# Output projection's last tile in two column quarters, a shorter expert choice, and rows of experts 1 to 11 gathered by DMA

## The chip, the cores and the metric

The kernel runs on one core of one Trainium2 chip. The metric is the device time of one execution in microseconds (us), taken as the median of repeated runs. Lower is better.

## The reference, cut to what matters

One layer of a hybrid decoder on 512 prompt tokens and 32 decode tokens (544 rows of width 1024, all float32). Attention and pooling branches are merged, then comes the output projection, a norm, a routed mixture of 32 experts of width 512 (top group of 4, then the best 2 of its 8 experts), and the residual sum:

```python
x = x + merged @ w['w_out']
hn = rms_norm(x, w['norm_ffn_g'])
g_w, g_idx = lax.top_k(softmax(hn @ w_route_group + b_g), 1)
top_l, top_i = lax.top_k(e_logits[group g_idx], 2)
comb = g_w * softmax(top_l)
# every token goes through its two experts:
y = (silu(xb @ w_gate[e]) * (xb @ w_up[e])) @ w_down[e]
x = x + sum over the two experts of comb * y
```

The weights of all 32 experts (6 MB each, 201 MB in all) have to come in from HBM, and an expert has some 34 of the 1088 token slots.

## The kernel before, in words

The program is written by hand with one instruction stream for each engine: TensorE (PE), VectorE (DVE), ScalarE (ACT), GpSimd (POOL) and SyncE (SP), which issues the loads of weights. Semaphores order the streams, and each stream runs strictly in the order of the code. Three stages matter here.

**Output projection and routing.** The token rows are five tiles: the decode tile first, then four prompt tiles of 128 rows (`ORDER`). The 1024 output columns are taken in halves of 512: half number 0 is the whole decode tile, halves 1 to 4 are the left halves of the four prompt tiles, 5 to 8 the right halves, and half 8 is called `LAST`. For each half PE runs `half_out` (8 products of 128 x 128 by 128 x 512 float32, 16 instructions in the trace, since a float32 product is two), DVE adds the residual (`add_out`), PE transposes the sum (`turn`), ACT or DVE copies the transpose out of PSUM, and PE forms routing logits from it (`route`). When both halves of a tile are there, DVE takes the reciprocal of the norm (`inverse2`), and then `choice` picks the group and the two experts by some twenty small dependent operations. From the choice PE computes each token's place in its experts' lists (`tile_ranks`), and DVE makes from it `mark`, one-hot tables `hot` and `hit` (`hits`); `tile_list` makes the lists of row numbers, `list_i`. The finished sums are also written to a table in HBM, `x2_rows`, and to the output `y`.

**How an expert gets its rows.** For experts in `SELECTED` PE multiplies a one-hot matrix with all token rows, which are kept in SBUF split into bfloat16 parts (`select`, 24 products of 512 columns and two float32 products), ACT copies the result out (`stage_x`) and PE transposes it (`turn_x`). For experts in `GATHERED` (2 to 8 before) POOL issues an indirect DMA that reads the rows of `x2_rows` by `list_i` (`gather_x`), and PE transposes what landed (`turn_gathered`). The row vector is then scaled by DVE (`take_x`). POOL's first gather waits until all of `x2_rows` is written (`base_written`) and the lists are there (`rows_listed`).

**Experts.** Each expert has three weight chunks of 2 MB: two for gate and up (`gate_up`), one for `down`. There are 96 chunks, and a ring of ten buffers (`CHUNK_AT`) in SBUF. SP issues chunk n + 10 once PE has used chunk n. Chunks 0 to 6 are issued when the projection begins, 7 to 9 when the projection's last data leave the places that the chunks overwrite. Chunks 10 and 11 are issued in four pieces each, as expert 0's first eight products free the buffers of chunks 0 and 1. POOL adds each expert's result to `y` by an indirect DMA (`add_y`). The part of a loop on DVE that follows expert 10 is a hardware loop.

## Time and profile before

| what | value |
|---|---|
| median of 3 runs | 976.71 us (975.9 to 978.06) |
| profiled execution | 975.49 us, of which the span of instructions is 973.7 us |
| PE busy | 935.4 us, 96% |
| DVE busy, ACT busy | 402.7 us, 241.4 us |
| HBM traffic | 260 MB, 268 GB/s over the span |

Times in the rows below are us from the span's start. PE's matmuls are pipelined, so their busy times overlap and a busy engine isn't one at its peak. "PEld" is PE's loading of weights. A wait is named by what released it.

### The profile page before, as it was taken

How to read it: one execution, taken by the hardware profiler on the slowest of the kernel's cores; microseconds unless marked ns; L12 is line 12 of the kernel's file. 1: busy time of each engine (PE TensorE's matmuls, PEld its weight loads, DVE VectorE, ACT ScalarE, POOL GpSimd, SP SyncE). 2: the span in 40 equal slices, each digit the busy share in tenths (PEclk: the TensorE clock that was granted, in tenths of full speed). 3: DMA queues.
4: the chain of work that ended last, by engine and by line, in shares of the span. 5: the costliest groups of instructions: out<-in, count | busy, mean ns of one | idle time of the engine just before them, and what ended most of it. 6: DMA issues, size and time to landing. Idle time of an engine off the chain costs nothing.

```text
span 973.7 us, 12332 instructions
## 1 busy us (share of the span) xinstructions
PE 935.4 (96%) x4804; PEld 506.4 (52%) x4804; DVE 402.7 (41%) x916; ACT 241.4 (25%) x600; POOL 70.6 (7%) x79
## 2 busy tenths in 40 slices
PE   5999999999999999999989999999999999999996
PEld 4555777777678888855444333333333333333331
DVE  4589688687543345553661242111111112111111
ACT  4432554454533100032221111111111111111111
POOL 0100001000000000002101111101101010110101
PEclk9999999999999999999999999999999999999999
DMA  9620412112112226369269999999999999999995
GB/s 330 217 87 24 149 55 84 44 44 87 44 44 86 87 87 229 140 255 409 113 221 385 393 393 415 423 418 417 422 416 423 419 415 424 417 423 420 425 416 181
DMA packets 33848, 255.17 MB, mean 262 GB/s; under 512 B 8241, under 2 KB 11569, under 8 KB 18792
## 3 DMA queue, kind: packets, MB, share of 16 engines
q1 hardware_dynamic: 28912, 242.45, 61.6%
q0 software_dynamic: 4880, 11.94, 4.4%
q8 instruction: 39, 0.64, 0.3%
q14 instruction: 17, 0.14, 0.0%
HBM read 245.91 MB, written 14.58 MB: 268 GB/s over the span
## 4 chain that ended last, share of the span: by engine, by line
PE 71%; DMA 20%; DVE 5%; ACT 1%; issue 1%; SPq 1%; POOL 0%; POOLq 0%; DVEq 0%; ACTq 0%
PE ps L1983 25%; DMA arena<-in_w_gu 19%; PE ps L2301 14%; PE ps L2328 7%; PE ps L1921 6%; PE ps L2142 4%; PE ps L2227 4%; PE ps L2068 1%; DMA arena<-in_x 1%; PE ps L2042 1%; PE ps L1999 1%; PE ps L2025 1%; PE ps L2271 1%; PE ps L2311 1%; PE ps L2302 1%
## 5 line engine op out<-in xcount | busy, mean ns | idle before, releaser
L1983 PE MATMUL ps<-arena 128*128 128x272 f32 x1120 | 266.7, 394 | 2.7 <-DVE arena L1395 1.0
L2301 PE MATMUL ps<-arena 128*64 128x512 f32 x512 | 229.7, 597 | 10.2 <-DMA arena<-in_w_gu 10.1
L1983 PEld LDWEIGHTS ps<-arena 128*128 128x128 f32 x1120 | 208.9, 190 | 52.3 <-issue 7.1
L2302 PE MATMUL ps<-arena 128*64 128x512 f32 x512 | 229.7, 597 | 0.0
L828 ACT ACTIVATE arena<-ps 128x272 f32<-128x272 f32 (+5 forms) x181 | 86.2, 483 | 364.7 <-PE ps L1983 167.6
L2301 PEld LDWEIGHTS ps<-arena 128*64 128x64 f32 x512 | 66.2, 137 | 141.5 <-issue 114.8
L1721 DVE SCALAR_TENSOR_TENSOR arena<-arena,list_w,ps 64x512 f32<-64x512 f32 x32 | 24.0, 749 | 217.9 <-ACT arena L1099 217.8
L2227 PE MATMUL ps<-arena 128*64 128x512 bf16 (+2 forms) x600 | 81.7, 421 | 0.9 <-DVE arena L1636 0.9
L1921 PE MATMUL ps<-arena 128*128 128x512 f32 (+1 forms) x192 | 74.1, 544 | 7.0 <-DVE arena L1187 7.0
L1099 ACT ACTIVATE arena<-ps,list_w 64x512 f32<-64x512 f32 x32 | 21.8, 682 | 202.3 <-PE ps L2302 202.2
L786 POOL DMA_INDIRECT out_y<-arena,list_i x32 | 45.2, 1414 | 362.4 <-DVE arena L1728 327.8
L2302 PEld LDWEIGHTS ps<-arena 128*64 128x64 f32 x512 | 66.2, 137 | 2.8 <-issue 2.8
L1717 DVE TENSOR_TENSOR arena<-ps,g_ffn 128x512 f32<-128x512 f32 x32 | 22.2, 692 | 100.0 <-PE ps L2271 94.3
L2328 PE MATMUL ps<-arena 128*64 128x512 f32 x256 | 61.1, 599 | 1.0 <-ACT arena L828 1.0
L2328 PE MATMUL ps<-arena,const 128*64 128x512 f32 x256 | 61.0, 598 | 0.5 <-ACT const L828 0.5
L2142 PE MATMUL ps<-arena 128*128 128x512 f32 x128 | 59.4, 602 | 0.0
L2227 PEld LDWEIGHTS ps<-arena 128*64 128x64 bf16 (+2 forms) x600 | 36.5, 116 | 40.6 <-issue 16.5
L1921 PEld LDWEIGHTS ps<-arena 128*128 128x128 f32 x192 | 38.1, 203 | 36.3 <-issue 33.7
L1728 DVE COPY arena<-ps 64x512 f32<-64x512 f32 x32 | 21.9, 683 | 49.9 <-PE ps L2328 49.9
L2142 PEld LDWEIGHTS ps<-arena 128*128 128x128 f32 x128 | 22.7, 190 | 21.7 <-issue 21.5
L928 ACT ACTIVATE arena<-arena,a_stat 128x256 f32<-128x256 f32 (+1 forms) x64 | 30.0, 471 | 14.9 <-DVE a_stat L1449 14.7
L2328 PEld LDWEIGHTS ps<-arena,const 128*64 128x64 f32 x256 | 16.9, 136 | 30.3 <-issue 29.4
(264 smaller groups left out, 772.2 us busy)
## 6 DMA issues: line engine op xcount, KB each, us to landing
arena<-in_w_gu SPq DMA_DIRECT2D x62, 2048.0 KB, 44.8
arena<-in_w_ed SPq DMA_DIRECT2D x30, 2048.0 KB, 47.1
arena<-in_w_pair SPq DMA_DIRECT2D x20, 1024.0 KB, 4.9
arena<-in_w_q SPq DMA_DIRECT2D x2, 2048.0 KB, 14.6
arena<-in_w_out SPq DMA_DIRECT2D x2, 2048.0 KB, 12.4
arena<-in_w_ed SPq DMA_DIRECT2D x8, 512.0 KB, 15.8
arena<-in_w_gu SPq DMA_DIRECT2D x8, 512.0 KB, 22.7
arena<-in_x SPq DMA_DIRECT2D x4, 512.0 KB, 10.0
```

Of the source, the lines that this page charges most:

```text
L786: pool.indirect_dma_start(out=o["y"], out_offset=bass.IndirectOffsetOnAxis(ap=index, axis=0), in_=y_rows[s][0:C, :], in_offset=None, compu ...
L828: return act.activation(out, in_, ACT.Copy)
L928: act.activation(p, p, ACT.Exp, bias=a_stat[:, s, 0, c:c + 1], accum_out=a_stat[:, s, 1, c:c + 1])
L1717: tt(xT[s], split(ps[:, x_bank(s), :], (JX, C)), over(g_ffn[:], C), ALU.mult).then_inc(xe_taken, 1)
L1721: stt(hid, silu, weight, ps[64:64 + C, 2 + s, :], ALU.mult, ALU.mult)\
L1921: ins = mm(ps[0:r, bank, 0:w], hU[:, k, t * P:t * P + r], slot(u, KD, w)[:, k, :], start=k == 0, stop=k == KD - 1)
L1983: ins = mm(out, w[:, k, :], tokens[:, k, :], start=k == 0 and q in "127", stop=k == 3, skip_group_check=q not in "127")
L2142: ins = mm(ps[:, out_bank(h), :], merged[:, k, t * P:(t + 1) * P], w_out[c][:, k, :], start=k == 0, stop=k == KD - 1)
L2227: ins = mm(ps[64 * c:64 * c + C, bank, :], places[0:r], rows[0:r, c * 512:(c + 1) * 512], start=j == 0, stop=j == NT - 1)
L2301: mm(ps[0:C, 2 + s, :], xT[s][:, j, :], w[:, jj, 1, :], start=j == 0, stop=j == JX - 1)
L2302: ins = mm(ps[64:64 + C, 2 + s, :], xT[s][:, j, :], w[:, jj, 0, :], start=j == 0, stop=j == JX - 1)
L2328: ins = mm(ps[64 * q:64 * q + C, 6 + s, :], hidT[s][:, j, :], w_down(n)[:, j, 512 * q:512 * q + 512], start=j == 0, stop=j == JH - 1)
```

## The change

1. `LAST` becomes two quarters of 256 columns, numbers 8 (`LAST`) and 9 (`END`), each with its own sum, transpose and logits. The right half of `w_out` lies in SBUF as two quarters, and ACT copies the merged rows of the last tile aside (`last_merged`), so that chunk 8 can be loaded over `merged` after half 7. Chunk 9 is loaded over the two quarters of `w_out` in two parts. The writes of the last half to `x2_rows` and `y` are issued behind both.
2. `choice` finds both expert maxima with one `max` instruction in place of a reduction, a masking and a second reduction, and the one-hot of both experts is made ahead of the other results.
3. The last prompt tile isn't selected and then transposed for expert 0. Its rows are multiplied as the stationary operand with a one-hot matrix `hot_last` of the places, which gives the transpose at once, added in PSUM to the transpose of the rest (`turn_first`). DVE makes `hot_last` straight after the choice (`last_hots`) from `chosen` and the ranks.
4. `GATHERED` is 1 to 11. Experts 1, 9, 10 and 11 lose their selection, and POOL gets four more gathers, the first of them for expert 1.
5. The exponentials of the choice on ACT stand behind the staging of expert 0.

```diff
-GATHERED = tuple(range(2, 9))
+GATHERED = tuple(range(1, 12))
...
-        w_out = [area(4096 * c, KD, 512) for c in range(2)]
+        w_left, w_quarter = area(0, KD, 512), area(4096, 2, KD, 256)
+        last_merged = area(52992, KD, P)
...
-        CHUNK_AT = [8192] + [19584 + 4096 * c for c in range(6)] + [0, 4096, 15488]
+        CHUNK_AT = [8192] + [19584 + 4096 * c for c in range(6)] + [0, 15488, 4096]
...
-            sp.wait_ge(out_ready, LAST + 1)
+            sp.wait_ge(out_ready, LAST)
             load_chunk(EARLY + 1)
-            sp.wait_ge(x2_ready, LAST + 1)
-            sp.dma_start(half_cols(x2_rows, LAST), x_half(LAST)).then_inc(last_written, 16)
-            sp.dma_start(half_cols(o["y"], LAST), x_half(LAST)).then_inc(last_written, 16)
-            load_chunk(N_CHUNK - 1)
+            part, e = chunk_of[N_CHUNK - 1]
+            for q in range(2):
+                sp.wait_ge(out_ready, LAST + q + 1)
+                sp.dma_start(w_up(N_CHUNK - 1)[:, 2 * q:2 * q + 2], a["w_gu"][expert_at(e), part][:, 2 * q:2 * q + 2])\
+                    .then_inc(chunk_in[N_CHUNK - 1], 16)
+            sp.wait_ge(x2_ready, END + 1)
+            sp.dma_start(half_cols(x2_rows, LAST), last_x2).then_inc(last_written, 16)
+            sp.dma_start(half_cols(o["y"], LAST), last_x2).then_inc(last_written, 16)
...
-            for e in range(-2, NE):
+            for e in range(-3, NE):
                 if e + 4 in GATHERED:
                     above(pool, xe_ready, max([g + 1 for g in GATHERED if g < e + 4 and g % 2 == e % 2], default=0))
                     gather_x(e + 4)
...
+                if h == 1:
+                    act.wait_ge(unit_merged, 8)
+                    copy(last_merged, merged[:, :, ORDER[NT - 1] * P:(ORDER[NT - 1] + 1) * P])
...
-                link(dve.tensor_reduce(m1, flat_allow, AX_X, ALU.max))
-                link(stt(e_t, allow, m1, e_rank, ALU.is_equal, ALU.mult))
+                link(dve.max(top[0:r, :], flat_allow))
+                stt(e_t, allow, top[0:r, 0:1], e_rank, ALU.is_equal, ALU.mult)
+                link(stt(e_t2, allow, top[0:r, 1:2], e_rank, ALU.is_equal, ALU.mult))
                 link(dve.tensor_reduce(b1, flat_e, AX_X, ALU.max))
-                ts(hots[0], e_t, b1, None, ALU.is_equal)
...
-                link(stt(allow, hots[0], NEVER, allow, ALU.mult, ALU.add))
-                link(dve.tensor_reduce(m2, flat_allow, AX_X, ALU.max))
...
+            def last_hots():
+
+                t = ORDER[NT - 1]
+                dve.wait_ge(rank_ready, NT)
+                stt(hot_last[:, 0, :], cc("place"), ps[:, 7, t * NE:t * NE + 1], chosen.to_broadcast((P, C)),
+                    ALU.subtract, ALU.is_equal).then_inc(hot_ready, 1)
...
+                if j == NT - 2:
+                    add_out(LAST)
                 choice(j)
+            last_mean()
+            add_out(END)
+            marks(NT - 2)
...
+            choice(NT - 1)
+            last_hots()
+            marks(NT - 1)
             hits(NT - 1)
...
+            def turn_first():
+
+                pe.wait_ge(x_staged, 1)
+                for j in range(JX // 2):
+                    mm(split(ps[:, x_bank(0), :], (2, JX // 2, C))[:, :, j, :], x_picked[0][:, j * P:(j + 1) * P], ident,
+                       start=j == 0, stop=False)
+                pe.wait_ge(hot_ready, NT)
+                for j in range(JX):
+                    ins = mm(ps[:, x_bank(0), j * C:(j + 1) * C], last_rows[:, j * P:(j + 1) * P], hot_last[:, 0, :],
+                             start=False, stop=j == JX - 1)
+                ins.then_inc(xe_ready, 1)
...
-            select(0, range(NT - 1))
-            select(1, range(NT - 2), 3)
+            select_first(0)
+            route(END)
+            for j in range(1, NT - 2):
+                select_first(j)
+            select_first(NT - 2).then_inc(picked, 1)
             tile_ranks(NT - 1)
-            pe.wait_ge(hot_ready, NT)
-            select(0, (NT - 1,)).then_inc(picked, 1)
-            select(1, (NT - 2,), 3)
+            tile_list(NT - 2)
+            pe.wait_ge(ssq2_ready, END + 1)
+            turn_first()
...
-            turn_rows(0)
-            select(1, (NT - 1,), 3).then_inc(picked, 1)
             tile_list(NT - 1)
             gate_up(0, 0, up_no(0, 0), (0, 0))
```

Two places show how this moves instructions. On PE, from the last half's logits to expert 0's first product, the program had before (L2227 are the selection's products, L2271 transposes expert 0's selected rows, L2184 to L2189 `tile_ranks`, L2198 `tile_list`, L2301 and L2302 `gate_up`):

```order
L2176 MATMUL ps<-arena 128x36 [waits first_logits,logits_taken,x2T_last]
L2227 MATMUL ps<-arena 64x512 [waits lower_ready,ssq2_ready,parts_taken,hot_ready]
L2227 MATMUL ps<-arena 64x512 x33
L2184 MATMUL ps<-first_place,cbf 128x32 [waits hit_ready]
L2189 MATMUL ps<-one_hot_bf,cbf 128x32 [waits choice_ready]
L2227 MATMUL ps<-arena 64x512 [waits hot_ready]
L2227 MATMUL ps<-arena 64x512 x7
L2271 MATMUL ps<-const,arena 128x2x64 [waits x_staged]
L2227 MATMUL ps<-arena 64x512 x2
L2198 MATMUL ps<-arena 64x32 [waits hit_ready]
L2301 MATMUL ps<-arena 64x512 [waits chunk_in0,xe_taken]
```

and it has now (L2316 is `select_first`, L2324 and L2328 `turn_first`, L2256 `tile_list`, L2396 `gate_up`, L2374 expert 1's gathered rows):

```order
L2316 MATMUL ps<-arena 64x512 [waits ssq2_ready,hot_ready,lower_ready,parts_taken]
L2235 MATMUL ps<-arena 128x36 [waits first_logits,logits_taken,x2T_last]
L2316 MATMUL ps<-arena 64x512 x5
L2247 MATMUL ps<-one_hot_bf,cbf 128x32 [waits choice_ready]
L2324 MATMUL ps<-const,arena 128x2x64 [waits x_staged,ssq2_ready]
L2328 MATMUL ps<-arena 128x64 [waits hot_ready]
L2328 MATMUL ps<-arena 128x64 x7
L2256 MATMUL ps<-arena 64x32 [waits hit_ready]
L2396 MATMUL ps<-arena 64x512 [waits chunk_in0,xe_taken]
L2374 MATMUL ps<-const,arena 128x64 [waits x_full1,rows_listed]
```

The selection is done ahead of the ranks, nothing of it stands behind them, and expert 1's transposes wait for a DMA (`x_full1`) where they waited for ACT.

On POOL, at the end of the projection, the queue had before (L775 and L776 write `x2_rows` and `y`, L793 gathers, L786 adds to `y`):

```order
L776 DMA out_y<-arena 128x512
L793 DMA arena<-x_rows,list_i 64x1024 [waits last_written,dec_written,half_moved3,rows_listed,half_moved2,zeros_set,half_moved1,half_moved0]
L793 DMA arena<-x_rows,list_i 64x1024
L793 DMA arena<-x_rows,list_i 64x1024 [waits xe_ready]
L786 DMA out_y<-arena,list_i 544x1024 [waits y_taken_act,y_taken_dve]
```

and it has now:

```order
L792 DMA out_y<-arena 128x512
L809 DMA arena<-x_rows,list_i 64x1024 [waits last_written,half_moved3,dec_written,half_moved2,rows_listed,half_moved1,half_moved0]
L809 DMA arena<-x_rows,list_i 64x1024
L809 DMA arena<-x_rows,list_i 64x1024 [waits xe_ready] x2
L802 DMA out_y<-arena,list_i 544x1024 [waits y_taken_act,y_taken_dve]
```

One gather more stands ahead of the first addition to `y`; the other three follow one each ahead of the additions of experts 5, 6 and 7.

## Rows read from the trace of the kernel before

**Rows 1.** The page: what the DMA engines moved, in 40 slices of the span.

```profile
GB/s 330 217 87 24 149 55 84 44 44 87 44 44 86 87 87 229 140 255 409 113 221 385 393 393 415 423 418 417 422 416 423 419 415 424 417 423 420 425 416 181
```

**Rows 2.** Waits of PE from 690 to 974: total us, times, longest.

```profile
PE ps L2301 <- DMA arena<-in_w_gu: 10.1, 13, 1.9
```

**Rows 3.** The chain that ended last, 885 to 974: start, us, what.

```profile
890.77 47.45 DMA arena<-in_w_gu
...
938.27 0.64 PE ps L2301
...
969.21 1.11 POOL out_y L786
```

**Rows 4.** SP's queue in order of time, 490 to 541: start, us, line.

```profile
509.44 2.90 SPq L706 DMA_DIRECT2D arena<-in_w_ed  x4
...
521.33 0.33 SPq L679 DMA_DIRECT2D arena<-in_w_gu  x1
```

**Rows 5.** Stretches: us, busy times, PEclk, DMA share, GB/s.

```profile
499.00:501.00 2.00, 2.00 (x12) 0.90 (x10) 1.76 (x9) 0.00 (x0) 0.00 (x0) 0.50 0.88 266
523.00:532.50 9.50, 9.34 (x57) 3.50 (x53) 2.32 (x4) 1.93 (x4) 1.56 (x2) 1.00 1.01 432
532.50:541.50 9.00, 9.00 (x48) 3.07 (x44) 1.44 (x2) 0.68 (x1) 1.73 (x2) 1.00 1.02 374
```

**Rows 6.** DMA queues, 532 to 590.15: packets, MB, share.

```profile
q1 hardware_dynamic: 1465, 21.30, 90.6%
q0 software_dynamic: 800, 1.48, 10.5%
```

**Rows 7.** DMA queues, 592 to 650.4.

```profile
q1 hardware_dynamic: 1640, 23.92, 96.0%
q0 software_dynamic: 337, 0.57, 5.0%
```

**Rows 8.** DVE in order of time around the last tile's choice.

```profile
489.47 0.25 DVE L1604 SCALAR_TENSOR_TENSOR const<-const,stat,r_bias 128x36 f32<-128x36 f32 x1
...
494.43 0.69 DVE L1560 TENSOR_TENSOR arena<-ps,arena 128x512 f32<-128x512 f32 x1
...
497.68 0.25 DVE L1604 SCALAR_TENSOR_TENSOR const<-const,stat,r_bias 128x36 f32<-128x36 f32 x1
...
499.39 0.19 DVE L1614 TENSOR_REDUCE arena<-arena 128x1 f32<-128x32 f32 x1
...
502.22 0.18 DVE L1629 TENSOR_TENSOR one_hot_bf<-a_stat 128x32 bf16<-128x32 f32 x1
...
507.40 0.69 DVE L1717 TENSOR_TENSOR arena<-ps,g_ffn 128x512 f32<-128x512 f32 x1 [2.20 <-PE ps L2271]
508.54 0.18 DVE L1797 TENSOR_SCALAR list_i<-ps 64x32 uint32<-64x32 f32 x1 [0.45 <-PE ps L2198]
```

**Rows 9.** PE in order of time, 489 to 518.

```profile
489.02 4.54 PE L2142 MATMUL ps<-arena 128*128 128x512 f32 x10
...
496.61 1.08 PE L2176 MATMUL ps<-arena 128*128 128x36 f32 x8 [0.47 <-DVE arena L1696]
...
498.04 5.55 PE L2227 MATMUL ps<-arena 96*64 96x512 bf16 x34
...
503.76 0.18 PE L2189 MATMUL ps<-one_hot_bf,cbf 128*128 128x32 bf16 x1
...
508.23 0.64 PE L2302 MATMUL ps<-arena 128*64 128x512 f32 x1
...
515.92 1.79 PE L2257 MATMUL ps<-arena 128*64 128x64 f32 x20
517.64 0.64 PE L2301 MATMUL ps<-arena 128*64 128x512 f32 x1
```

**Rows 10.** POOL in order of time, 509 to 530.

```profile
509.78 1.03 POOL L793 DMA_INDIRECT arena<-x_rows,list_i  x1 [22.83 <-issue]
```

**Rows 11.** The gathers' line, 500 to 525.

```profile
DMA to landing us min/median/max: 5.9/6.8/7.7
```

More of the change, by code:

```diff
@@ L503, in build @@
         wide = take(2, NE)
-        g_max, g_best, e_max1, e_best1, e_max2, e_best2 = (take(1) for _ in range(6))
+        g_max, g_best, e_best1, e_best2 = (take(1) for _ in range(4))
+        spare = CONST["before"][0] + (NT - 1) * (NG + NE)
+        top = const[:, spare:spare + 8]
+        chosen = const[:, spare + 8:spare + 9]
+        e_tmp2 = split(const[:, spare + 9:spare + 9 + NE], (NG, EG))
         g_diff, g_exp = take(NT, NG), take(NT, NG)
@@ L1076, in _ @@
             take_parts(0)
-            for h in range(1, LAST + 1):
+            for h in range(1, END + 1):
                 square(h)
-                if h >= NT:
-                    root2(h - NT + 1)
-                if h < LAST:
+                if h >= NT and h != LAST:
+                    root2(h - NT + 1 if h < LAST else NT - 1)
+                if h < END:
                     take_turned(h)
@@ L1633, in first_hots @@
             def first_hots(j):
-                out = hot[:, :, j, :] if j < NT - 1 else hot_last
-                tt(out, across(cc("place"), 2), over(mark[:, j, 0:2], C), ALU.is_equal).then_inc(hot_ready, 1)
+                tt(hot[:, 0:1, j, :], across(cc("place"), 1), over(mark[:, j, 0:1], C), ALU.is_equal).then_inc(hot_ready, 1)
+            def last_hots():
+                t = ORDER[NT - 1]
+                dve.wait_ge(rank_ready, NT)
+                stt(hot_last[:, 0, :], cc("place"), ps[:, 7, t * NE:t * NE + 1], chosen.to_broadcast((P, C)),
+                    ALU.subtract, ALU.is_equal).then_inc(hot_ready, 1)
             def one_hots(s, marks):
@@ L1644, in hot_places, with marks @@
             def hot_places(e, turn, s):
-                dve.wait_ge(picked, turn - 1)
+                above(dve, picked, turn - 1)
                 one_hots(s, mark[:, :, e:e + 1] if isinstance(e, int) else mark[:, :, bass.ds(e, 1)])
-            def hits(j):
+            def marks(j):
                 t = ORDER[j]
@@ L1671, in _ @@
             link(dve.memset(e_diff, 0.0))
[L1673 removed]
+            add_out(0)
             half_mean(0)
@@ L1684, in _ @@
                 if j == 3:
+                    marks(0)
                     hits(0)
-            for j in range(1, NT):
-                add_out(j, 1)
+            for j in range(1, NT - 1):
+                add_out(half_no(j, 1))
                 if j == 1:
@@ L2141, in half_out @@
                 for k in ks:
-                    ins = mm(ps[:, out_bank(h), :], merged[:, k, t * P:(t + 1) * P], w_out[c][:, k, :],
-                             start=k == 0, stop=k == KD - 1)
+                    rows = merged[:, k, t * P:(t + 1) * P] if h < LAST else last_merged[:, k, :]
+                    w = w_left[:, k, :] if c == 0 else w_quarter[:, :, k, :] if h < LAST else w_quarter[:, h - LAST, k, :]
+                    ins = mm(ps[:, out_bank(h), 0:width(h)], rows, w, start=k == 0, stop=k == KD - 1)
                 if ks[-1] == KD - 1:
@@ L2172, in route @@
                 at = 36 * t if c == 1 else 36 * (NT + t)
-                ks = range(KD) if h == 0 else range(4 * c, 4 * c + 4)
+                ks = range(KD) if h == 0 else range(4 * c, 4 * c + 4) if h < LAST else range(2 * h - 12, 2 * h - 10)
+                first, last = (ks[0], ks[-1]) if h < LAST else (4, KD - 1)
                 for k in ks:
-                    rows = dec_x2T[:, k, :] if h == 0 else x2T[(h - 1) % 2][:, k % 4, :]
-                    ins = mm(ps[0:ROWS[t], 6, at:at + 36], rows, w_route[:, k, :], start=k == ks[0],
-                             stop=k == ks[-1])
+                    rows = dec_x2T[:, k, :] if h == 0 else x2T[(h - 1) % 2][:, (k - ks[0]) % 4, :]
+                    ins = mm(ps[0:ROWS[t], 6, at:at + 36], rows, w_route[:, k, :], start=k == first, stop=k == last)
                 ins.then_inc(logit_ready, 1)
@@ L2205, in _ @@
             dec_out()
-            for h in range(1, 2 * NT - 1):
+            for h in range(1, LAST):
                 half_out(h, (0, 1, 2) if h == 1 else (0,))
```

160 lines of the change are left out of this document (100 added, 60 removed).

## The prediction, made before the changed kernel ran

> **What bounds the kernel now.** I read the page first. Its line of what the DMA engines moved [rows 1] is low and uneven while the projections run, dips twice before the experts begin (113 and 221 GB/s, from about 463 to 511 us), and from slice 22 of 40 on stays at 385 to 425 GB/s to the last slice but one. The reader is to see that the second half is one long stream of weights. The stretches say how full it is: from 523 to 532.5 the engines' share is 1.01 at 432 GB/s [rows 5]. I take 431 GB/s as the undisturbed rate, so a 2.097 MB chunk takes 4.87 us. PE looks as busy as the DMA engines there, so the next view is PE's waits: from 690 on it waits 10.1 us in 13 waits for `in_w_gu` [rows 2], so PE is the faster of the two and has at least that in hand. The chain that ended last says the same: at 938.27 expert 30's second gate and up chunk lands, issued 47.45 us before, and the last addition to `y` is issued at 969.21 by a chain of PE, ACT and DVE behind it [rows 3]. This tail is the same in both kernels, since experts 30 and 31 are selected in both.
>
> When does the stream begin? All ten buffers are full by then, and SP's queue issues the first piece of chunk 10 at 509.44, 1.2 us into expert 0's products, which begin at 508.23; chunk 12 goes out at 521.33, behind the first half of expert 1's, which begin at 517.64 [rows 4, 9]. Two chunks from 509.44 take 9.7 us, and with two gathers and the first latency they end at about 521, so chunk 12 comes just in time. From 509.44 to the end 86 chunks have to pass: 86 x 4.87 = 419 us, plus what else uses the engines. So the time is the moment at which expert 0 frees its first buffer, plus the stream, plus the tail. PE's work between is hidden under the stream.
>
> **What a gather costs the stream.** Two stretches of nearly equal length tell it. From 532 to 590.15 five experts pass with five gathers and five additions to `y`; queue 1, the weights, moves 21.30 MB [rows 6]. From 592 to 650.4 four experts pass with four additions and no gather, and it moves 23.92 MB [rows 7]. At 431 GB/s the stretches could hold 25.06 and 25.17 MB. The first lost 3.76 MB or 8.7 us, the second 1.25 MB or 2.9 us. An addition so costs 0.73 us of stream, and a gather (8.7 - 5 x 0.73) / 5 = 1.02 us. Bounds: queue 0's share grows from 5.0% of 58.4 us to 10.5% of 58.15 us, 6.1 against 2.9 us, which gives 0.49 us for a gather; the dearest stretch, 532.5 to 541.5, moved 374 GB/s, which less queue 0's 0.34 MB (a fifth of its part in [rows 6] rounded up) is 3.03 MB of weights, or 7.0 of 9 us, 2.0 lost and 1.26 for the gather [rows 5].
> A rule stands against that. The Trainium skill, DMA: Bandwidth & Descriptors (Anatomy of one DMA), gives the part of a DMA that grows with size as bytes over 436 GB/s; some 34 rows of 4 KB would then take about 0.32 us, an estimate by the page. The same page (Queues, rings and completion order) has each engine take turns between rings packet by packet, which fits a loss above the bytes. The trace has 1.02 us, and I go by it.
>
> **The change part by part.**
> *Quarters.* PE's last half is 16 instructions, of which ten take 4.54 us from 489.02 on [rows 9], 0.43 us each, so it ends at 493.6. With 256 columns each is 0.21 us. The first quarter then ends some 3.4 us sooner than the half did, and 0.3 more because the choice before it is shorter: about 489.8. DVE adds it (0.4 us, a 512-column sum takes 0.69 [rows 8]) and starts tile 2's choice at 490.2, where it started at 489.47. That is 0.7 us later. The old kernel had DVE busy with that choice until the sum at 494.43; the new one is at 494.9. Then come the second sum (0.4), the marks, a 256-column copy and the hits of tile 2, but PE's transposes run under the marks. The last choice starts at about 497.05 instead of 497.68: 0.6 us gained.
> *Choice.* From its first operation to `one_hot_bf` it took 502.22 - 497.68 = 4.54 us [rows 8]. Operations that depend on each other follow 0.19 to 0.31 us apart. Gone from ahead of the one-hot are a reduction, a masking, a product and four unlinked ones; one linked and one unlinked product are new. I count 3.56 us. `max` itself has no row: 0.19 us if it is like the reduction of 32 columns at 499.39 [rows 8], 0.4 if twice that; I take 0.22. Its end is at 5.04 us, because `chosen` adds two linked operations. The one-hot is thus there at 500.8 and DVE free at 502.1.
> *Last tile.* In the old kernel the ranks' last product ran at 503.76, held by the selection (34 products, 5.55 us from 498.04), followed by marks, hot, ten products, ACT's copy, transposes, and `take_x` at 507.40; expert 0 began at 508.23 [rows 8, 9]. Now DVE makes `hot_last` at 502.1 to 502.3. PE's 16 instructions of 64 columns follow at 0.11 to 0.13 us, as the eight of the logits at 496.61 do (1.08 us, [rows 9]): 1.9 us, to 504.2. With 0.05 us of hand-over, `take_x` (0.69) and 0.1, expert 0 begins at 505.1. **The start is 3.1 us earlier.** The four products ahead of `hot_last` lie in PE's idle time; if that cover is gone they cost 1 us.
> *Clock.* From 499 to 501 PE's granted clock was 0.50, that is 1.2 GHz, after PE had had only small operations from the end of half 8 at 493.6 to the selection at 498.04; it fell on that selection [rows 5, 9]. Now PE has next to nothing between 499 and 502.3, and what follows is `turn_first` and expert 0's products, both on the path. Nothing lost if the clock stays up; a stretch of 3.4 us at half speed costs 1.7. I take 1.0 us. The Trainium skill, TensorE: Matmul & The Clock Gate (What's actually happening), says that throttled is the default state and activity releases it, which is the direction of this row.
> *Expert 1's gather.* `list_i` is made at 508.54 and the first gather is issued at 509.78, about 1.06 us behind its end; gathers land 5.9 to 7.7 us after [rows 8, 10, 11]. Now `list_i` comes right behind `take_x`, at 505.05 to 505.2, the gather goes at 506.3 and lands at 512.2 to 514.0. Expert 1's transposes are wanted at 512.1 (505.1 plus the 517.64 - 508.23 = 9.4 us between the two experts, less the 1.8 us of list products at 515.92 and 0.6 of transposes [rows 9]). So it is just in time or 1.9 us late. Queued behind the wait are the list products and expert 1's products, which free chunk 12's buffer: at 518.2 to 520.1 against 521.33. The stream has chunks 10 and 11 and by then three gathers until about 519. I charge nothing. I don't expect `base_written` to hold it, since the last half's write is issued behind the sum that ends at 495.3, eleven us before.
> *Chunks 8 and 9 earlier, `last_merged`, exponentials, memset.* The DMA engines have room before 509 [rows 1], and ACT is busy for 241 of 974 us, so nothing; all ten chunks were already in time.
> *Selections removed.* 26 products each, 4.2 us at the 5.55 / 34 = 0.16 us of [rows 9]; all of it lies under the stream: nothing, as PE waited for chunks anyway.
> *Gathers added.* Four: 4 x 1.02 = 4.1 us (2.0 to 5.0). Nothing hides them, as the engines are full whenever they run.
>
> **Sum.** -3.1 + 1.0 + 4.1 = +2.0 us. The profiled execution, 975.49 us (span 973.7), becomes 977.5; it lies 1.2 us below the median of the runs, so the forecast is 978.7. With the ends of the terms (start -4.0 to -2.0, clock 0 to 1.7, gathers 2.0 to 5.0, expert 1 0 to 1.5) it is -2.0 to +6.2; all at one end together is unlikely.
>
> **Rivals.** A measurement of this kernel can tell some 0.2%, 2 us, from no change.
> *A, the forecast (0.64):* the gathers cost more than the start brings. Own range 976.7 to 981.0. About half of it is above +2 us, half within 2 us.
> *B, faster by cheap gathers (0.20):* a gather costs its bytes alone, 34 x 4 KB at 431 GB/s = 0.32 us, the rest of the loss of [rows 6] being something that rapid use of buffers brings, and the clock stays up: -3.1 + 1.3 = -1.8, 974.9 us. For it speaks queue 0's low share, against it the recovery to 432 GB/s between the gathers [rows 5]. It decides, with the clock up, from a gather below 0.3 us. The page's 436 GB/s gives the same.
> *C, expert 1 starves the stream (0.12):* its gather is the first and lands late, since the write of the last half or the first pieces of chunk 10 are ahead of it. If it is 5 us late, chunk 12 is 4 us late, 3 after the slack: 982 us.
> *D, PE's saving counts (0.04):* if PE were the bound, the three later selections less would give -3.1 - 12.6, about 961 us. The DMA share of 1.01 speaks against it.
>
> Chances: slower is half of A and C, 0.44; same is the other half of A and a little of B, 0.35; faster 0.21. The range 974.5 to 982.3 leaves out D and the outer parts of B and C.
>
> **What would show it.** The first piece of chunk 10 goes out near 506.3 (before 509.44); `choice` is a microsecond shorter to the one-hot; PE's waits for `in_w_gu` start well before 690 and sum to over 20 us; a stretch with gathers of experts 9 to 11 moves some 8% less of weights than one without; the granted clock is 0.50 somewhere from 500 to 509. I am wrong if the later gathers leave the chunks' rate alone (then faster), or if PE stands between experts 0 and 1 for more than 3 us (then slower than forecast).

## The result, and the profile after

The changed kernel takes **979.11 us** (median of 20 runs, 975.96 to 982.48), the kernel before 976.84 us in the same session (20 runs, 973.01 to 979.83). The ratio is 1.0022, with a 95% interval of 1.0012 to 1.0033: 2.2 us slower, 1.2 to 3.2. The forecast was 978.7 us.

The profiled execution took 981.4 us, 2.3 above its median, and its span is 979.6. So what came before the change must first be lined up. From the page (busy time, what the DMA engines moved in 40 slices, the chain by line):

```profile
PE 932.4 (95%) x4756; PEld 509.0 (52%) x4756; DVE 399.2 (41%) x909; ACT 240.5 (25%) x600; POOL 73.3 (7%) x82
...
GB/s 323 221 86 12 161 49 89 44 44 87 43 44 86 87 86 239 127 273 410 143 205 375 392 392 399 409 424 418 420 420 420 422 413 425 419 418 425 417 422 153
...
DMA arena<-in_w_gu 28%; PE ps L2040 25%; PE ps L2396 10%; PE ps L1978 6%; PE ps L2201 5%; PE ps L2423 5%; PE ps L2298 2%; PE ps L2125 1%; DMA arena<-in_x 1%; PE ps L2099 1%; PE ps L2056 1%; PE ps L2082 1%; PE ps L2235 1%; DVE arena L1449 1%; PE ps L2374 1%
```

The dip before the experts remains (143 and 205 GB/s where [rows 1] has 113 and 221), and the second half is again one stream. PE in order of time, first of the kernel before, then of the changed one:

```profile
470.37 5.40 PE L2142 MATMUL ps<-arena 128*128 128x512 f32 x12
```

```profile
471.76 5.40 PE L2201 MATMUL ps<-arena 128*128 128x512 f32 x12
...
489.61 1.97 PE L2201 MATMUL ps<-arena 128*128 128x256 f32 x8
...
501.63 0.19 PE L2247 MATMUL ps<-one_hot_bf,cbf 128*128 128x32 bf16 x1 [1.38 <-DVE one_hot_bf L1659]
...
502.09 1.54 PE L2324 MATMUL ps<-const,arena 128*128 128x128 f32 x8
503.42 3.51 PE L2328 MATMUL ps<-arena 128*128 128x64 f32 x16
...
507.79 1.11 PE L2396 MATMUL ps<-arena 128*64 128x512 f32 x1 [0.29 <-DVE arena L1776]
...
511.26 1.06 PE L2396 MATMUL ps<-arena 128*64 128x512 f32 x1
...
512.96 0.60 PE L2396 MATMUL ps<-arena 128*64 128x512 f32 x1
...
517.36 0.71 PE L2374 MATMUL ps<-const,arena 64*128 64x64 f32 x8
```

The first row in each is the same piece of work, 12 of the 16 float32 instructions of one half, 13 us before the first quarter. It starts 1.39 us later after the change. That isn't the change's doing: the distance from the first products of the projection is the same (423.83 to 470.37, and 425.21 to 471.76), and before_fill (below), which has the old program up to there, starts it at 472.32. So I call this piece the **mark** and count all times from it. The mark-to-piece and mark-to-chunk times below repeat to 0.01 us between runs that differ only behind chunk 12 and have the same clock (before and before_extra6, after_fill and fill_g1to6, after_sel1 and sel1_g2to6), which is what makes this a fair ruler.

DVE in order of time around the last choice:

```profile
490.76 0.42 DVE L1587 TENSOR_TENSOR arena<-ps,arena 128x256 f32<-128x256 f32 x1 [0.68 <-PE ps L2201]
491.10 0.25 DVE L1638 SCALAR_TENSOR_TENSOR const<-const,stat,r_bias 128x36 f32<-128x36 f32 x1
...
497.88 0.26 DVE L1638 SCALAR_TENSOR_TENSOR const<-const,stat,r_bias 128x36 f32<-128x36 f32 x1
...
499.59 0.20 DVE L1648 MAX8 const<-arena 128x8 f32<-128x32 f32 x1
...
501.38 0.19 DVE L1659 TENSOR_TENSOR one_hot_bf<-a_stat 128x32 bf16<-128x32 f32 x1
...
502.83 0.29 DVE L1678 SCALAR_TENSOR_TENSOR arena<-const,ps 128x64 f32<-128x64 f32 x1
...
507.05 0.69 DVE L1776 TENSOR_TENSOR arena<-ps,g_ffn 128x512 f32<-128x512 f32 x1 [2.99 <-PE ps L2328]
507.65 0.17 DVE L1856 TENSOR_SCALAR list_i<-ps 64x32 uint32<-64x32 f32 x1
```

SP's queue (start, us, line), which answers to [rows 4]:

```profile
490.75 4.46 SPq L707 DMA_DIRECT2D arena<-in_w_gu  x2
...
509.81 4.56 SPq L723 DMA_DIRECT2D arena<-in_w_ed  x4
514.90 2.90 SPq L723 DMA_DIRECT2D arena<-in_w_gu  x4
523.41 0.33 SPq L692 DMA_DIRECT2D arena<-in_w_gu  x1
```

From the mark, the first piece of chunk 10 goes out after 38.05 us (39.07 before), chunk 12 after 51.65 (50.96 before). So the stream starts 1.0 us sooner, and 13.6 us later it is 0.7 us late. The stretches show why (us, busy times of PE, PEld, DVE, ACT, POOL, PEclk, DMA share, GB/s):

```profile
499.00:502.70 3.70, 2.32 (x25) 1.50 (x22) 3.32 (x20) 1.88 (x2) 0.00 (x0) 1.00 0.53 199
502.70:506.10 3.40, 3.40 (x19) 3.40 (x18) 1.26 (x7) 0.32 (x2) 0.00 (x0) 0.50 0.00 0
506.10:509.50 3.40, 3.11 (x12) 1.68 (x14) 2.22 (x11) 0.00 (x0) 0.70 (x1) 0.50 0.00 0
509.50:513.00 3.50, 3.50 (x12) 0.98 (x10) 0.28 (x2) 0.00 (x0) 1.29 (x2) 0.51 0.69 206
513.00:517.00 4.00, 4.00 (x22) 1.23 (x18) 0.00 (x0) 0.00 (x0) 0.00 (x0) 1.00 0.92 287
592.00:650.40 58.40, 50.88 (x258) 17.96 (x256) 9.06 (x14) 6.63 (x12) 8.98 (x7) 1.00 1.01 407
```

From 502.7 to 513 PE's granted clock is 0.50, the 1.2 GHz level, where [rows 5] has it from 499 to 501. It fell at the end of a stretch of 3.7 us in which PE was busy for 2.32 and waited 1.38 us for the one-hot, about a microsecond after that wait had ended. `turn_first`'s 16 instructions took 3.51 us from 503.42, and each product pair of expert 0 starts 0.85 us behind the last until 512.96, and 0.43 behind it from there on. The DMA engines stand still from 502.7 to 509.5 (share 0.00): all ten buffers are full, so the stream waits until this slow stretch has freed the first one.

The gathers of POOL, in time, and how long the first two took to land:

```profile
508.80 1.03 POOL L809 DMA_INDIRECT arena<-x_rows,list_i  x1 [21.31 <-DVE list_i L1856]
510.13 0.96 POOL L809 DMA_INDIRECT arena<-x_rows,list_i  x1 [0.30 <-issue]
518.83 0.93 POOL L809 DMA_INDIRECT arena<-x_rows,list_i  x1 [7.74 <-PE ps L2374]
```

```profile
DMA to landing us min/median/max: 3.2/4.0/4.7
```

PE's waits from 600 on (total us, times, longest) and the DMA queues from 592 to 650.4 (packets, MB, share), which answer to [rows 2] and [rows 7]:

```profile
PE ps L2396 <- DMA arena<-in_w_gu: 13.8, 20, 1.3
PE ps L2423 <- issue: 5.2, 3, 2.9
```

```profile
q1 hardware_dynamic: 1564, 22.81, 93.8%
q0 software_dynamic: 568, 0.96, 7.1%
```

PE waits 13.8 us for gate and up chunks (10.1 before) and 5.2 more where nothing is named, at the down products; the first is at 620.9 to 623.86. PE does less and waits more, and the end is no earlier. From 592 to 650.4 the stretch above has a DMA share of 1.01, 407 GB/s, and PE busy for 50.9 of 58.4 us. The weights queue moved 22.81 MB, where [rows 7] has 23.92: 1.11 MB or 2.6 us at 431 GB/s. That is for the two gathers issued in it, the rest of one issued at 589.16, and one addition to `y` more (five, where the kernel before has four).

### The profile page after: what moved, and what is told of

It reads as the page before. It is cut to its first block, busy times and chain, and to the rows that moved or that the text cites. A ratio compares the mean times of both kernels' runs of the same rounds, so it can differ in the third digit from the quotient of the medians.

```text
span 979.6 us, 12241 instructions
## 1 busy us (share of the span) xinstructions
PE 932.4 (95%) x4756; PEld 509.0 (52%) x4756; DVE 399.2 (41%) x909; ACT 240.5 (25%) x600; POOL 73.3 (7%) x82
## 4 chain that ended last, share of the span: by engine, by line
PE 63%; DMA 29%; DVE 4%; ACT 1%; issue 1%; SPq 1%; POOL 0%; POOLq 0%; DVEq 0%; ACTq 0%
DMA arena<-in_w_gu 28%; PE ps L2040 25%; PE ps L2396 10%; PE ps L1978 6%; PE ps L2201 5%; PE ps L2423 5%; PE ps L2298 2%; PE ps L2125 1%; DMA arena<-in_x 1%; PE ps L2099 1%; PE ps L2056 1%; PE ps L2082 1%; PE ps L2235 1%; DVE arena L1449 1%; PE ps L2374 1%
## 5 line engine op out<-in xcount | busy, mean ns | idle before, releaser
L2396 PE MATMUL ps<-arena 128*64 128x512 f32 x512 | 233.1, 602 | 14.2 <-DMA arena<-in_w_gu 13.8
L2040 PEld LDWEIGHTS ps<-arena 128*128 128x128 f32 x1120 | 208.9, 190 | 52.3 <-issue 7.1
L2397 PE MATMUL ps<-arena 128*64 128x512 f32 x512 | 233.2, 602 | 0.0
L843 ACT ACTIVATE arena<-ps 128x272 f32<-128x272 f32 (+5 forms) x178 | 84.2, 479 | 364.1 <-PE ps L2040 168.4
L2396 PEld LDWEIGHTS ps<-arena 128*64 128x64 f32 x512 | 66.4, 138 | 152.6 <-issue 118.5
L1978 PE MATMUL ps<-arena 128*128 128x512 f32 (+1 forms) x192 | 75.2, 550 | 6.5 <-DVE arena L1215 6.5
L2397 PEld LDWEIGHTS ps<-arena 128*64 128x64 f32 x512 | 66.4, 138 | 0.0
L2423 PE MATMUL ps<-arena 128*64 128x512 f32 x256 | 61.2, 599 | 4.3 <-issue 3.3
L2298 PE MATMUL ps<-arena 128*64 128x512 bf16 (+1 forms) x480 | 63.8, 414 | 0.0
L2201 PE MATMUL ps<-arena 128*128 128x512 f32 (+1 forms) x144 | 59.9, 554 | 0.0
L1978 PEld LDWEIGHTS ps<-arena 128*128 128x128 f32 x192 | 39.0, 208 | 36.2 <-issue 33.3
L2298 PEld LDWEIGHTS ps<-arena 128*64 128x64 bf16 (+1 forms) x480 | 29.1, 114 | 31.4 <-issue 12.0
L2201 PEld LDWEIGHTS ps<-arena 128*128 128x128 f32 x144 | 25.6, 190 | 19.8 <-issue 19.1
L2423 PEld LDWEIGHTS ps<-arena 128*64 128x64 f32 x256 | 16.9, 136 | 33.8 <-issue 32.2
## 6 DMA issues: line engine op xcount, KB each, us to landing
arena<-in_w_ed SPq DMA_DIRECT2D x8, 512.0 KB, 14.4
arena<-in_w_gu SPq DMA_DIRECT2D x8, 512.0 KB, 22.5
arena<-in_x SPq DMA_DIRECT2D x4, 512.0 KB, 10.5
```

Source lines behind the costliest of these rows:

```text
L843: return act.activation(out, in_, ACT.Copy)
L1978: ins = mm(ps[0:r, bank, 0:w], hU[:, k, t * P:t * P + r], slot(u, KD, w)[:, k, :], start=k == 0, stop=k == KD - 1)
L2040: ins = mm(out, w[:, k, :], tokens[:, k, :], start=k == 0 and q in "127", stop=k == 3, skip_group_check=q not in "127")
L2201: ins = mm(ps[:, out_bank(h), 0:width(h)], rows, w, start=k == 0, stop=k == KD - 1)
L2298: ins = mm(ps[64 * c:64 * c + C, bank, :], places[0:r], rows[0:r, c * 512:(c + 1) * 512], start=j == 0, stop=j == js[-1])
L2396: mm(ps[0:C, 2 + s, :], xT[s][:, j, :], w[:, jj, 1, :], start=j == 0, stop=j == JX - 1)
```

## The experiments

The two theories behind most runs: **G**, the weights' stream is the bound from expert 0 on and each gather takes about a microsecond of it; **K** (the expectations below call it theory C, which is not the prediction's rival C), the clock's fall eats what the earlier start brings. The rivals: the gathers cost their bytes alone, expert 1 starves the stream, or PE's saving counts. Ratios are against the kernel before on the same chip (medians 977.13 to 977.45 us beside the experiments), with 95% intervals; "first piece" and "chunk 12" are counted from the mark, "to the end" is from chunk 12's issue to the end of the span.

| run | median us | ratio | first piece | chunk 12 | to the end | gathers behind chunk 12 |
|---|---|---|---|---|---|---|
| before | 976.84 | 1 | 39.07 | 50.96 | 452.4 | 5 |
| after | 979.11 | 1.0022 (1.0012 to 1.0033) | 38.05 | 51.65 | 456.2 | 8 |
| after_g1to8 | 976.21 | 0.9995 (0.9981 to 1.0009) | 37.78 | 50.15 | 453.7 | 5 |
| after_fill | 977.83 | 1.0008 (0.9996 to 1.0019) | 35.68 | 47.64 | 456.2 | 8 |
| before_g2to11 | 981.81 | 1.0050 (1.0031 to 1.0070) | 40.36 | 52.26 | 457.8 | 8 |
| before_g2to5 | 974.62 | 0.9975 (0.9964 to 0.9986) | 37.80 | 49.69 | 451.8 | 2 |
| fill_g1to6 | 970.81 | 0.9939 (0.9924 to 0.9954) | 35.69 | 47.65 | 449.4 | 3 |
| after_sel1 | 977.82 | 1.0000 (0.9989 to 1.0011) | 35.92 | 47.82 | 457.0 | 8 |
| fill_old_choice | 979.68 | 1.0028 (1.0017 to 1.0039) | 37.35 | 49.30 | 456.5 | 8 |
| before_fill | 975.79 | 0.9984 (0.9967 to 1.0000) | 37.78 | 49.68 | 454.1 | 5 |
| before_extra6 | 983.81 | 1.0067 (1.0050 to 1.0084) | 39.06 | 50.95 | 459.9 | 11 |
| sel1_g2to6 | 970.75 | 0.9935 (0.9913 to 0.9958) | 35.92 | 47.82 | 452.8 | 3 |

The last three columns are of one profiled execution each, and "to the end" scatters: before and before_fill differ by 1.7 us in it, fill_g1to6 and sel1_g2to6 by 3.4, each pair with the same number of gathers. So the price of a gather is taken from the ratios.

Some of these runs take selections from PE or give it some. What one costs shows in the kernel before, for expert 9, at full clock:

```profile
607.05 3.19 PE L2227 MATMUL ps<-arena 96*64 96x512 bf16 x24
610.07 1.89 PE L2328 MATMUL ps<-arena,const 128*64 128x512 f32 x8
```

These are 24 instructions (20 bfloat16 products, and two float32 ones of two instructions each), and the next work starts 3.0 us after the first of them. Three selections are 9 us of PE's time.

**after_g1to8**: the changed kernel with experts 9, 10 and 11 selected by PE again.

```diff
-GATHERED = tuple(range(1, 12))
+GATHERED = tuple(range(1, 9))
```

> The changed kernel with experts 9, 10 and 11 selected again, so gathers for 1 to 8 alone. Theory G (a gather takes 1.0 us from a stream of weights that is always full, and PE's time is hidden): 3 gathers less, about 3.1 us faster than the changed kernel, 976.0 us, ratio to the kernel before 0.999. Rival P (PE's selections count, the gathers are hidden): three selections of 3 us more on PE, up to 9 us slower than the changed kernel, 988 us. Rival S (the whole loss of the change lies at the start, before expert 1's products): no difference to the changed kernel, 979 us.

Three gathers less took the ratio from 1.0022 to 0.9995: 2.6 us, 0.9 each, though PE does 9 us more. PE's waits for gate and up chunks sank from 13.8 to 9.3 us. This speaks for G, but not purely: in the profiled executions the fall of the clock was shorter too, and chunk 12 went out 1.5 us sooner. The clock was at 0.50 for 6.8 us in this one (10.2 in that of after), so the length of the fall isn't fixed, and the two kernels' profiles alone can't part the two theories.

**after_fill**: the changed kernel with 28 bfloat16 products on constants, into an unused PSUM bank, in PE's idle places: 6 before the transposes of the last quarter, 16 before the last ranks, 6 before expert 0. Their results are not used.

```diff
+            def fill(n):
+                for _ in range(n):
+                    mm(ps[:, 3, 0:256], ones_bf, cbf[:, :], start=True, stop=True)
...
+            pe.wait_ge(ssq2_ready, LAST)
+            fill(6)
             turn(END)
...
+            fill(16)
             tile_ranks(NT - 1)
...
+            fill(6)
             gate_up(0, 0, up_no(0, 0), (0, 0))
```

> The changed kernel with 28 small bfloat16 products of 256 columns into an unused PSUM bank in PE's idle times (6 ahead of the last quarter's transposes, 16 ahead of the wait for the last choice, 6 ahead of expert 0's products). The output is the same. Theory C (the granted clock of 0.50 from 502.7 to 513.0 costs 1.7 us in the last tile's products and 2.5 in expert 0's): the clock stays at 1.00, the first piece of chunk 10 is issued near 507 instead of 509.8, chunk 12 at 520 to 521 instead of 523.4, and the time falls by 2 to 3 us to 976.5. Rival: the clock falls anyway or the products only add work: 979 to 980 us.

The stretches, PE in order of time and SP's queue of this run:

```profile
499.00:502.70 3.70, 3.70 (x38) 2.52 (x34) 3.28 (x18) 1.88 (x2) 0.00 (x0) 1.00 0.63 233
502.70:506.10 3.40, 3.40 (x32) 3.26 (x31) 1.95 (x10) 0.32 (x2) 0.00 (x0) 1.00 0.02 7
506.10:509.50 3.40, 3.40 (x20) 1.36 (x20) 2.13 (x11) 0.00 (x0) 1.72 (x2) 1.00 0.19 34
509.50:513.00 3.50, 3.50 (x18) 1.15 (x16) 0.00 (x0) 0.00 (x0) 0.28 (x1) 1.00 1.01 302
```

```profile
472.09 5.40 PE L2201 MATMUL ps<-arena 128*128 128x512 f32 x12
...
500.18 1.92 PE L2335 MATMUL ps<-cbf 128*128 128x256 bf16 x16
...
503.72 1.90 PE L2328 MATMUL ps<-arena 128*128 128x64 f32 x16
...
506.65 0.64 PE L2404 MATMUL ps<-arena 128*64 128x512 f32 x1
```

```profile
507.77 2.90 SPq L723 DMA_DIRECT2D arena<-in_w_ed  x4
...
519.73 0.33 SPq L692 DMA_DIRECT2D arena<-in_w_gu  x1
```

The clock stays at 1.00, `turn_first`'s products take 1.90 us, as forecast, and from the mark the first piece goes out 2.4 us and chunk 12 4.0 us sooner than in after. The tail from chunk 12 is the same 456.2. In the medians the fillers bring only 1.3 us, where 2 to 3 were expected, and the intervals of after and after_fill overlap. The mean granted clock of every execution points to why. Of the 20 of after, nine have 0.987 or 0.988, the profiled one among them; they take 980.5 us in the mean. The six with 0.992 or more take 977.3. Of the 12 of after_fill none is below 0.990. So the profiled execution of after is one of its slower-clocked ones, and the fall there costs more than in the median. Where in the span the other executions lost their clock is not recorded. K stands, with its size between 1.3 us (median) and 4.0 us (the profiled pair).

**before_g2to11**: the kernel before with experts 9, 10 and 11 gathered.

```diff
-GATHERED = tuple(range(2, 9))
+GATHERED = tuple(range(2, 12))
```

> The kernel before with experts 9, 10 and 11 gathered too, nothing else. Theory G: 3 gathers more at 1.0 us each, 979.9 us, ratio 1.003. Rival P: three selections less on PE, up to 9 us faster. Rival S: no difference to the kernel before.

It is slower by 4.9 us, 1.6 for each of three gathers (1.0 was expected), although PE does 9 us less. If PE were the bound it would be far faster: that rival falls. In the profiled execution 1.3 us of it is a longer fall of the clock (6.8 us from 497.0, where before had 3.4), seen at the first piece. If the timed runs are like it, the rest is 3.6 us or 1.2 each.

**before_g2to5**: the other way, experts 6, 7 and 8 selected by PE.

```diff
-GATHERED = tuple(range(2, 9))
+GATHERED = tuple(range(2, 6))
```

> The kernel before with gathers for experts 2 to 5 alone, so 3 gathers less and 3 selections more. Theory G: 3.1 us faster as long as PE keeps ahead of the stream; PE's slack from 690 on was some 10 us and 3 selections take 9 to 12, so 973.8 to 975 us. Rival P: 9 us slower, 986 us.

It is faster by 2.4 us. A stretch of it:

```profile
600.00:700.00 100.00, 100.00 (x554) 37.48 (x552) 17.45 (x33) 15.10 (x27) 8.88 (x7) 1.00 1.01 420
...
800.00:900.00 100.00, 100.00 (x550) 37.36 (x550) 18.45 (x35) 15.35 (x28) 9.84 (x7) 1.00 1.01 419
```

PE is busy for all 100 of 100 us and no longer waits for a chunk: here PE has become the bound. That is the other end of the trade. It also had no fall of the clock near 500, which is 1.3 us at the first piece, so if the timed runs are like the profiled ones, only about 1 us is left for the three gathers less.

**fill_g1to6**: both findings together, the fillers and gathers for experts 1 to 6 only.

```diff
-GATHERED = tuple(range(1, 12))
+GATHERED = tuple(range(1, 7))
```

> The changed kernel with the 28 filling products and gathers for experts 1 to 6 alone. Theory G with C: five gathers less than after_fill (977.8 us), at 1.0 to 1.3 us each, if PE keeps ahead of the stream: 971.5 to 972.8 us, ratio 0.995, faster than both kernels. If PE becomes the bound, as in before_g2to5, some 974 us. Rival S (start only): no difference to after_fill.

By the ratios it is 6.0 us faster than before and 6.7 faster than after_fill, 1.35 for each of the five gathers, somewhat more than expected. PE's waits from 600 on:

```profile
PE ps L2404 <- DMA arena<-in_w_gu: 3.4, 4, 2.1
```

3.4 us in 4 waits, all behind 800, where after has 13.8 in 20: PE and the stream now end nearly together.

**after_sel1**: the changed kernel with expert 1 selected beside expert 0, in PE's idle time, in place of its gather, and no fillers. The last tile's part of expert 1 (two float32 products, four instructions) stands behind `turn_first`. The lines that make its one-hot tables on DVE and stage its rows on ACT are left out here.

```diff
-GATHERED = tuple(range(1, 12))
+GATHERED = tuple(range(2, 12))
...
+                    for c in range(2):
+                        mm(ps[64 * c:64 * c + C, 3, :], hot[0:r, 1, j, :], rows[0:r, c * 512:(c + 1) * 512],
+                           start=j == 0, stop=False)
...
+            pe.wait_ge(hot_ready, NT + 1)
+            for c in range(2):
+                ins = mm(ps[64 * c:64 * c + C, 3, :], hot_last[:, 1, :], last_rows[:, c * 512:(c + 1) * 512], start=False, stop=True)
+            ins.then_inc(picked, 1)
```

> The changed kernel with expert 1 selected as in the kernel before: its 20 products of the first four tiles run beside expert 0's into another PSUM bank, and its two float32 products of the last tile ahead of expert 0's first. Gathers are 2 to 11. Theory G: one gather less, 1.0 to 1.3 us. Theory C: the additional products lie in PE's idle time and keep the granted clock up, or shorten its fall from 10 us; up to 3 us more. So 975.5 to 978 us, and chunk 12 is issued at 519 to 521 instead of 523.4. Rival E (expert 1's selection was what held the old start, so its removal is the gain): chunk 12 later than 523.4 and 980 us or more.

No fall: the clock is 1.00 from 495.5 to 517, and the first piece goes out 35.92 us from the mark, 0.24 behind the run with fillers. So it is the removal of expert 1's selection that emptied PE ahead of `turn_first` and let the clock fall: none of the five profiled executions with fillers or with this selection has the fall, both without them (after, after_g1to8) have it. The four instructions more behind `turn_first` cost a quarter of a microsecond. That one gather less gives it back (1.0000 against 1.0008) is not shown, as the intervals overlap.

**fill_old_choice**: after_fill with the choice's operations of the kernel before.

```diff
-                link(dve.max(top[0:r, :], flat_allow))
-                stt(e_t, allow, top[0:r, 0:1], e_rank, ALU.is_equal, ALU.mult)
-                link(stt(e_t2, allow, top[0:r, 1:2], e_rank, ALU.is_equal, ALU.mult))
+                link(dve.tensor_reduce(m1, flat_allow, AX_X, ALU.max))
+                link(stt(e_t, allow, m1, e_rank, ALU.is_equal, ALU.mult))
...
+                link(stt(allow, hots[0], NEVER, allow, ALU.mult, ALU.add))
+                link(dve.tensor_reduce(m2, flat_allow, AX_X, ALU.max))
```

> after_fill with the old operations of the choice (two reductions, the masking, the one-hot made behind the rest but ahead of the products with the token number), all else as changed. Expected: the last choice's one-hot comes 0.9 us later behind its start, the start of the choice 0.3 later, expert 0's first product 1.0 to 1.3 us later than in after_fill, the first piece of chunk 10 near 508.9, and 978.9 us. Rival: the choice isn't on the path, no difference in the issue of chunk 10.

The first piece is 1.67 us later from the mark, chunk 12 1.66, the median 1.85. That is more than expected: the last choice takes 0.83 us longer to its one-hot and, since the choices before it are longer too, starts 1.14 us later instead of 0.3. The choice is most of what the start gains.

**before_fill**: the kernel before with 14 fillers, 10 before the last half's transposes and 4 before its logits.

```diff
+            pe.wait_ge(ssq2_ready, LAST)
+            fill(10)
             turn(2 * NT - 2)
...
+            fill(4)
             route(2 * NT - 2)
```

> The kernel before with 14 filling products (10 behind half 8, 4 ahead of its logits) into an unused PSUM bank. Theory C: the fall of the granted clock at 498.3 for 3.4 us doesn't occur, the selection of 34 products takes 4.3 us instead of 5.5 and expert 0 begins about 1 us sooner; 976.1 us, ratio 0.999. Rival: the fall is not tied to PE's idle time and comes anyway; no difference.

No fall either, the first piece at 37.78 from the mark in place of 39.07, and by the ratio 1.6 us below the kernel before, with an interval that ends at 1.0000. before_g2to5 has no fall and no fillers, and its first piece is at 37.80. So the old kernel's own fall of 3.4 us costs 1.3 where it occurs; that the fillers prevent it is not shown by one execution, since it stays out without them too. Both programs with the clock up part by 37.78 - 35.68 = 2.1 us; the other 1.3 of the start is the old kernel's fall, which the changed one trades for a longer one.

**before_extra6**: the kernel before with six more gathers, for experts 9 to 14, whose rows nobody reads; PE's work is unchanged. Ahead of each, POOL also waits until the last gather into the same buffer has landed.

```diff
+EXTRA = tuple(range(9, 15))
...
-                if e + 4 in GATHERED:
+                if e + 4 in GATHERED + EXTRA:
...
+                    if e + 4 in EXTRA:
+                        pool.wait_ge(x_full[e % 2], 16 * len([g for g in GATHERED + EXTRA if g < e + 4 and g % 2 == e % 2]))
```

> The kernel before with six more gathers, for experts 9 to 14, whose rows nobody uses: these experts are selected on PE as before, and POOL waits for the landing of the buffer's last gather ahead of each. PE's work is unchanged. Theory G (the gather itself takes the stream's time): 6 x 1.0 to 1.3 = 6.0 to 7.8 us slower, 984 us, ratio 1.007. Rival Q (not the gather but PE's faster pace in the gathered experts lowers the rate of the weights): no difference. Rival bytes alone (0.32 us each): 2 us slower.

It is 6.4 us slower (983.81 against 977.42), 1.07 a gather, or 0.8 to 1.4 by the ends of the interval. From the mark the first piece and chunk 12 stand where they stood (39.06, 50.95), so all of it is in the stream. Its stretches, PE's waits from 600 on and, from 592 to 650.4, its DMA queues:

```profile
600.00:700.00 100.00, 95.98 (x518) 35.20 (x518) 16.97 (x33) 14.51 (x26) 13.83 (x12) 1.00 1.01 407
700.00:800.00 100.00, 96.01 (x526) 34.96 (x522) 17.27 (x32) 14.81 (x26) 8.44 (x6) 1.00 1.01 420
```

```profile
PE ps L2304 <- DMA arena<-in_w_gu: 14.4, 20, 1.7
```

```profile
q1 hardware_dynamic: 1494, 21.76, 91.8%
q0 software_dynamic: 707, 1.32, 9.0%
```

Share 1.01 with and without gathers, but 407 GB/s from 600 to 700 with them and 420 from 700 on without; queue 1 moved 2.16 MB less than in [rows 7], 5.0 us for the five gathers issued in the stretch. PE waits 14.4 us for gate and up chunks, where the kernel before has 10.1, and its other waits are the same. This is the cleanest proof of G: beside the gathers only POOL's own waits were added.

**sel1_g2to6**: after_sel1 with gathers for experts 2 to 6 only, no fillers.

```diff
-GATHERED = tuple(range(2, 12))
+GATHERED = tuple(range(2, 7))
```

> after_sel1 with gathers for experts 2 to 6 alone, no filling products. Theory G: five gathers less than after_sel1 (977.8 us) at 1.0 to 1.3 us, and PE's slack, 15.0 us of waits for weights there, holds four of the five selections of 3 us: 971.5 to 973 us, ratio 0.994 to 0.996. If PE becomes the bound: 974 us.

970.75 us, as fast as fill_g1to6, a little faster than expected, and free of work that nobody uses. From the mark it repeats after_sel1 to the hundredth (35.92, 47.82). Both of these beat the kernel before by 0.6%.

## Why the prediction was right, and where its terms were off

**The bound: right.** before_extra6 and before_g2to11 settle it: more gathers lengthen the time whether PE gains by them or not. The rival "PE's saving counts" has no run for it down to five gathers; only with four, two of them behind chunk 12 (before_g2to5), does PE bind. Its price was also too large: a selection is 22 products and not 26, and the row that gave 4.2 us for it was 3.4 of 5.55 us at the lower clock. At full clock it is 3.0 us, so three are 9 us and not 12.6.

**The gathers, +4.1 us: right, somewhat small.** Five pairs of runs differ in gathers while the stream binds: (2.6 + 6.5 + 4.9 + 6.7 + 6.4) / (3 + 6 + 3 + 5 + 5) = 27.1 / 22 = 1.23 us each, taken from the ratios, with 0.9 to 1.6 in a single pair. Where a pair differs in its fall of the clock too, that is in it. The forecast had 1.02, with bounds of 0.49 and 1.26. The pure one is 1.07. Four are so 4.3 to 4.9 us. Only three of the four stand behind chunk 12, though (3.2 to 3.7 us). "Nothing hides them" is not shown for the fourth, expert 1's, which was issued at 508.80 while the engines stood still; no run prices it alone. The rival of 0.32 us is refuted, and with it the estimate by the bytes.
The Trainium skill, DMA: Bandwidth & Descriptors (Bandwidth, Measured), also lists 0.95 us for 64 KB and 6.15 for 1 MB through GpSimd's path; between them the 136 KB of 34 rows would be 1.34 us, an estimate by that table. The 1.07 us of before_extra6 are nearer to it than to the bytes over 436 GB/s.

**The start, -3.1 us: right only with the clock up.** With fillers the first piece goes out 3.39 us sooner than in [rows 4], from the mark. The steps inside, lined up by 1.39 us: the last choice started at 496.49 in the time of [rows 8] (forecast 497.05), the one-hot came 3.50 us behind it (3.56), `max` took 0.20 us (0.22), `hot_last` was begun at 501.44 (502.1), `turn_first`'s products take 1.90 us at full clock (1.9). What I hadn't parted is where the 3.39 comes from. 1.67 is the choice (fill_old_choice), 1.3 is the old kernel's own fall of the clock (before_fill), and quarters, last tile and list together are left with 0.4. The forecast had 0.6 for the quarters, 1.0 for the choice and so 1.5 for the last tile; the last tile's share was mostly the old fall, since the selection that held the ranks ran at half speed for 3.4 of its 5.55 us. Most of the restructuring gains little once the clock is equal.

**The clock, +1.0 us (0 to 1.7): too small, and the term that was mis-sized.** I had one stretch of 3.4 us at half speed in mind. It was 10.2 us in the profiled execution, and PE's work in it lay on the path: `turn_first` took 3.51 us in place of 1.9, expert 0's first products the rest. That is 2.4 us at the first piece and 4.0 at chunk 12, against a forecast ceiling of 1.7. In the medians it is 1.4 us (1.0022 against 1.0008), within the forecast's bounds. The two differ because the fall varies between executions: 6.8 us in after_g1to8's, and the one profiled of after lies 2.3 us above its median with one of the lowest mean clocks of the 20. What sets the length is open. I had also looked only for the gap between 499 and 502.3 and not asked what fills it: after_sel1 shows that the removed selection of expert 1 did.
The Trainium skill, TensorE: Matmul & The Clock Gate (What's actually happening), has the throttled level as the default and activity as what releases it; the runs agree, as fillers and a real selection both keep the clock at 1.00 where the changed kernel has 0.50. Why it then stayed at 0.50 through 10.2 us of a nearly always busy PE, no run here shows.

**The sum.** With terms as measured: -3.4 for the start, +4.3 to +4.9 for the gathers, +1.4 for the clock give +2.3 to +2.9, where 2.2 was measured and 2.0 forecast. after_fill, the same without the clock, comes to +0.9 to +1.5 by the terms and measures +0.8; with three gathers in place of four the terms would give -0.2 to +0.3, which its interval of -0.4 to +1.9 doesn't exclude. That the sum lies 0.2 us from the measured one is partly luck: the start brought 0.3 more than forecast, gathers and clock cost up to 0.8 and 0.4 more, the signs cancel, and the ratio's own interval is 2 us wide.

**Expert 1, nothing: right.** `list_i` at 507.65, the gather at 508.80, landed after 3.2 us, at 512.0; its transposes start at 517.36 behind PE's own products. In after_fill the gather goes at 507.48 and takes 5.9 us, so it lands at 513.4; the transposes start at 513.67, straight behind expert 0's products and without a wait. "Just in time" holds there, with 0.3 us in hand. The rival that expert 1 starves the stream falls.

**The signs.** PE's waits start at 621 and sum to 13.8 us for gate and up and 19.0 with the waits at the down products for which nothing is named; over 20 was foretold. A stretch with gathers moved 4.6% less of weights, not 8%: it held two gathers and the rest of a third, not one every 11.6 us as where they all run. The first piece went out at 509.81 and not near 506.3: by the mark that is 508.42, and 506.05 with the clock up.

## What to carry to other kernels

Where a stream of weights fills the DMA engines, price every other transfer in microseconds of that stream, and give work to the compute engine up to the point at which it would bind (here five and six gathers were the best tried, against eight and eleven; at four, in the kernel before, PE binds). Before you take work out of an engine's idle time, look whether that work keeps its clock up ahead of a part on the path: a gap is not free if what follows it runs at half speed. And line up two profiles by a piece of work that the change doesn't touch before you read differences of a microsecond.

## What the runs showed of the hardware that was not expected

- A gather of some 34 rows of 4 KB takes 1.07 us out of a full stream (before_extra6; 0.9 to 1.6 by pair), over three times the 0.32 us that its bytes take at 431 GB/s, while the DMA share stays at 1.01.
- The same gather lands 3.2 to 4.7 us after its issue where the engines stood still until just then (the first two of after), 5.9 to 7.7 where chunk 10's pieces go out beside it ([rows 11]), and 8.3 to 8.6 us (issues at 587.6 and 599.1 of before_extra6) under the stream.
- The granted clock stayed at 0.50 through 10.2 us although PE was busy for 3.40, 3.11 and 3.50 us of its three stretches (3.4, 3.4 and 3.5 us); before it fell PE had been busy for 2.32 of 3.7 us. With the fillers PE was busy for all 3.70 of that stretch, and the clock stayed at 1.00.
- `max`, which gives the eight greatest of 32 columns on 128 partitions, takes 0.20 us, as much as one reduction (0.19).
